# Reordering VectorE's sums at the seam between two MLP products, and the last rows' products and roots

## What is computed

```python
h = rmsnorm(x, g_pre_mlp[i]) * (1.0 + scale_f) + shift_f
y = jnp.square(jax.nn.relu(h @ w_mlp_in)) @ w_mlp_out      # 2048 -> 8192 -> 2048
x = x + gate_f * rmsnorm(y, g_post_mlp[i])
```

## Time and profile before

| | us |
|---|---|
| Median of 3 runs (lowest, highest) | 2253.55 (2251.96, 2254.7) |
| The profiled execution: device time | 2250.02 |
| Its span in the profile | 2248.2 |
| Mean granted TensorE clock | 0.986 |
| Busy: TensorE / VectorE / ScalarE / GpSimd | 2162.1 / 1511.6 / 862.5 / 391.1 |
| Second MLP product begins (first half of P1) | 1611.66 |
| Tail on VectorE: start of moving P5 out, end of the last row | 2225.19, 2243.72 |

### The profile page before, as it was taken

How to read it: one execution, slowest core, us unless ns; L and a number is a source line. 1 busy time by engine, 2 the same in 40 slices (tenths; PEclk the granted TensorE clock), 3 DMA queues, 4 the chain that set the end, 5 groups by cost and what they waited for, 6 DMA issues and landing times.

```text
span 2248.2 us, 26316 instructions
## 1 busy us (share of the span) xinstructions
PE 2162.1 (96%) x9751; PEld 1766.1 (79%) x9751; DVE 1511.6 (67%) x1459; ACT 862.5 (38%) x1076; POOL 391.1 (17%) x217
## 2 busy tenths in 40 slices
PE   4789999999999998999999999999999999999996
PEld 3568888887777887788888888888788888888875
DVE  6967666666767634665445444544688989898998
ACT  6333333331333224444344335334434444344443
POOL 1000000000000001000000000000054545463654
PEclk9899999999999999999999999999999999999998
DMA  9946654753454352566666646746455664567663
GB/s 366 354 163 217 200 185 133 235 162 115 153 168 136 119 182 74 192 220 225 201 202 220 224 171 206 250 159 202 131 187 180 239 236 166 190 233 243 236 237 138
DMA packets 262305, 441.16 MB, mean 196 GB/s; under 512 B 18156, under 2 KB 110512, under 8 KB 256184
## 3 DMA queue, kind: packets, MB, share of 16 engines
q1 hardware_dynamic: 261376, 435.45, 57.6%
q10 hardware_dynamic: 824, 4.27, 0.5%
HBM read 379.88 MB, written 59.79 MB: 196 GB/s over the span
## 4 chain that ended last, share of the span: by engine, by line
PE 80%; issue 8%; DVE 5%; DMA 3%; ACT 1%; POOL 1%; DVEq 1%; SPq 1%; POOLq 0%; ACTq 0%
PE pair L730 25%; PE pair L732 25%; PE pair L731 25%; DVE am_acc L1749 3%; DMA am_item<-in_w_ada 2%; DVE v_op L1976 1%; PE pair L827 1%; DMA w_raw<-in_w_in 1%; PE pair L801 1%; DVEq L1748 1%; POOL v_raw L2198 0%; PE pair L818 0%; PE pair L1014 0%; PE pair L867 0%; PE pair L876 0%
## 5 line engine op out<-in xcount | busy, mean ns | idle before, releaser
L730 PE MATMUL pair<-in_hi,w_hi 128*128 128x512 f32 x1792 | 723.6, 404 | 7.8 <-DVE in_lo L1766 6.2
L732 PE MATMUL pair<-in_hi,w_lo 128*128 128x512 f32 x1792 | 701.9, 392 | 0.0
L731 PE MATMUL pair<-in_lo,w_hi 128*128 128x512 f32 x1792 | 701.0, 391 | 0.0
L1509 DVE TENSOR_TENSOR w_lo<-w_raw,w_hi 128x2048 fp32r<-128x2048 f32 (+1 forms) x142 | 292.1, 2057 | 405.4 <-ACT w_hi L1107 405.0
L1107 ACT ACTIVATE w_hi<-w_raw 128x2048 fp32r<-128x2048 f32 (+1 forms) x142 | 244.8, 1724 | 461.6 <-PE pair L732 418.4
L730 PEld LDWEIGHTS pair<-in_hi,w_hi 128*128 128x128 f32 x1792 | 338.6, 189 | 87.2 <-issue 18.6
L732 PEld LDWEIGHTS pair<-in_hi,w_lo 128*128 128x128 f32 x1792 | 337.7, 188 | 72.9
L731 PEld LDWEIGHTS pair<-in_lo,w_hi 128*128 128x128 f32 x1792 | 338.7, 189 | 70.0 <-issue 2.6
L730 PE MATMUL pair<-v_op,hid_r 128*128 128x512 f32 x896 | 350.0, 391 | 5.8 <-DVE hid_r L1952 4.5
L732 PE MATMUL pair<-v_op,hid_r 128*128 128x512 f32 x896 | 349.5, 390 | 0.0
L731 PE MATMUL pair<-v_op,hid_r 128*128 128x512 f32 x896 | 349.5, 390 | 0.0
(11 more groups left out here) (202 smaller groups left out, 1882.8 us busy)
## 6 DMA issues: line engine op xcount, KB each, us to landing
w_raw<-in_w_mlp_in SPq DMA_DIRECT2D x64, 1024.0 KB, 5.3
v_raw<-in_w_mlp_out SPq DMA_DIRECT2D x128, 512.0 KB, 5.0
hid_r<-hid_scratch SPq DMA_DIRECT2D x112, 512.0 KB, 6.5
hid_scratch<-hid_r SPq DMA_DIRECT2D x28, 1792.0 KB, 6.5
am_item<-in_w_ada SPq DMA_DIRECT2D x64, 512.0 KB, 7.7
w_raw<-in_w_in SPq DMA_DIRECT2D x128, 256.0 KB, 3.6
af_item<-in_w_ada SPq DMA_DIRECT2D x64, 512.0 KB, 4.8
w_raw<-in_w_in SPq DMA_DIRECT2D x128, 128.0 KB, 3.5
```

Of the source, the lines that this page charges most:

```text
L730: pe.matmul(dst, a[0], b[0], start=start, stop=False, skip_group_check=onto)
L731: pe.matmul(dst, a[0], b[1], start=False, stop=False, skip_group_check=onto)
L732: return pe.matmul(dst, a[1], b[0], start=False, stop=stop, skip_group_check=onto)
L1509: dve.tensor_tensor(w_lo[n][:, view], w_raw[n][:, view], w_hi[n][:, view].bitcast(F32), ALU.subtract)\
```

## The change

At the seam, on VectorE: part 1 of the low parts of `hid_r` (of block 15) comes ahead of the sums; half 5's split comes next. B11 - B12 and B22 - B12 are made in halves of 128x1024 by a new `seam_b12`, and `seam_sum` orders itself by a drain in place of a wait on `t_dve`. GpSimd's products for `y_t2` (columns 2 and 0) move from unit 14 to behind unit 15's sums, and a third one (column 3), which VectorE made, goes to GpSimd between the two roots. The roots of row blocks 2 and 3, and of 0 and 1, are made in pairs. In the tail `out_row(0, 2)` comes ahead of adding the last product P4, and the last squares of C12 may start one `add` earlier.

```diff
--- before.py
+++ after.py
@@ -1464,7 +1464,8 @@
                     .then_inc(o_sq, 1)
 
             def finished(u):
-                return (ev_x, u + 1), (ev_y, 2 * u + 2), (ev_y, 2 * u + 2), (ev_q, 2 * u + 3)
+                c12 = (ev_w, UNITS + 1) if u == UNITS - 1 else (ev_y, 2 * u + 2)
+                return (ev_x, u + 1), c12, (ev_y, 2 * u + 2), (ev_q, 2 * u + 3)
 
             SQUARES = []
             for dc, u in ((0, U_DC0), (1, UNITS - 1)):
@@ -1954,9 +1955,10 @@
                     if b == LAST and part == 0:
                         split_operand(3)
                         split_operand(4)
-                        b12_sums(0, False)
-                        seam_sum(0)
-                        split_operand(5)
+                if b == LAST:
+                    split_operand(5)
+                    seam_b12(0)
+                    seam_sum(0)
 
             for b in range(FBS):
                 for mm in range(MM_O if b == 0 else 0, MM_O):
@@ -1991,11 +1993,22 @@
                     dve.tensor_tensor(v_raw[q[B11]][:, :, :], v_raw[q[B11]][:, :, :], v_raw[q[B12]][:, :, :],
                                       ALU.subtract).then_inc(t_dve, 1)
 
+            def seam_b12(h, third=False):
+                q = raw_at[0]
+                b11, b12, b22 = [v_raw[q[role]][:, h, :] for role in (B11, B12, B22)]
+                if third:
+                    return dve.tensor_tensor(b12, b22, b12, ALU.subtract)
+                if h == 0:
+                    done, count = raw_arrived(0, B12)
+                    dve.wait_ge(done, count)
+                    dve.wait_ge(v_lo, product_end(P1))
+                return dve.tensor_tensor(b11, b11, b12, ALU.subtract)
+
             def seam_sum(h):
                 q = raw_at[0]
                 done, count = raw_arrived(0, B22)
                 dve.wait_ge(done, count)
-                dve.wait_ge(t_dve, 1)
+                dve.drain()
                 dve.tensor_tensor(v_sum[:, h, :], v_raw[q[B22]][:, h, :], v_raw[q[B11]][:, h, :], ALU.add)\
                     .then_inc(t_seam, 1)
 
@@ -2032,7 +2045,10 @@
                 elif p == P5:
                     dve.wait_ge(ev_w, u + 1)
                     dve.wait_ge(ev_q, 2 * u + 2)
-                    add(c12, False)
+                    if u == UNITS - 1:
+                        add(c12, False).then_inc(ev_w, 1)
+                    else:
+                        add(c12, False)
                     add(c22, False).then_inc(ev_y, 1)
                 elif u < UNITS - 1:
                     add(c21, False).then_inc(ev_q, 1)
@@ -2046,10 +2062,14 @@
                     gate_row(Q_GF + FBS // 2 - 1, FBS // 2 - 1, bank[3])
                     hidden(LAST)
                 elif i not in (4, 5):
+                    if i == 6:
+                        seam_b12(1).then_inc(t_dve, 1)
                     split_operand(i)
                 if i == 6:
                     seam_sum(1)
-                    b12_sums(0, True)
+                    seam_b12(0, True)
+                if i == 7:
+                    seam_b12(1, True).then_inc(t_dve, 1)
                 while i - 4 >= product_end(evicted) - 1:
                     add_product(evicted)
                     evicted += 1
@@ -2070,7 +2090,8 @@
                 evicted += 1
 
             def total(t):
-                dve.tensor_reduce(ss4[:, t:t + 1], ss[:, t * CG:(t + 1) * CG], AX_X, ALU.add).then_inc(o_ss, 1)
+                rows = ss[:, t * CG:(t + 2) * CG].rearrange("p (t c) -> p t c", t=2)
+                dve.tensor_reduce(ss4[:, t:t + 2], rows, AX_X, ALU.add).then_inc(o_ss, 1)
 
             def out_row(n, t):
                 x1 = v_raw[raw_at[UNITS][ROLE_OF_T[t]]]
@@ -2084,25 +2105,21 @@
 
             dve.wait_ge(o_sq, 12)
             total(2)
-            total(3)
             gain(y_t1[:, :, 3, :], 3)
-            dve.wait_ge(o_sq, 14)
-            gain(y_t2[:, :, 3, :], 3)
+            dve.wait_ge(o_mul, 2)
+            dve.drain()
+            dve.wait_ge(o_rstd, 1)
+            out_row(0, 2)
             add_product(7 * UNITS - 1)
-            dve.wait_ge(o_mul, 4)
+            out_row(1, 3)
+            dve.wait_ge(o_sq, 16)
+            total(0)
+            gain(y_t2[:, :, 1, :], 1)
+            dve.wait_ge(o_mul, 5)
             dve.drain()
             dve.wait_ge(o_rstd, 2)
-            out_row(0, 2)
-            for t in range(2):
-                dve.wait_ge(o_sq, 15 + t)
-                total(t)
-                part = y_t2[:, t, 1, :]
-                dve.tensor_tensor(part, part, gg[:, 512:1024], ALU.mult)
-            out_row(1, 3)
-            dve.drain()
-            for t in range(2):
-                dve.wait_ge(o_rstd, 3 + t)
-                out_row(2 + t, t)
+            out_row(2, 0)
+            out_row(3, 1)
 
 
         @block.gpsimd
@@ -2208,11 +2225,13 @@
                 if u == U_DC0 + 1:
                     times_gain(y_t1, 0, 4)
                     times_gain(y_t1, 2, 4)
-                    times_gain(y_t2, 2, 8)
-                    times_gain(y_t2, 0, 8)
-            for n, t in enumerate((2, 3, 0, 1)):
-                pool.wait_ge(o_ss, n + 1)
-                inverse_root(rstd[:, t:t + 1], ms[:, t:t + 1], ss4[:, t:t + 1], D).then_inc(o_rstd, 1)
+            times_gain(y_t2, 2, 8)
+            times_gain(y_t2, 0, 8)
+            pool.wait_ge(o_ss, 1)
+            inverse_root(rstd[:, 2:4], ms[:, 2:4], ss4[:, 2:4], D).then_inc(o_rstd, 1)
+            times_gain(y_t2, 3, 14)
+            pool.wait_ge(o_ss, 2)
+            inverse_root(rstd[:, 0:2], ms[:, 0:2], ss4[:, 0:2], D).then_inc(o_rstd, 1)
 
 
 # ---- launch: one core; inputs and outputs as the reference has them ----
```

## The result

| | before | after |
|---|---|---|
| Median of 20 runs each, side by side (lowest, highest) | 2252.26 (2250.53, 2255.11) | 2257.26 (2254.61, 2261.16) |
| Ratio, 95% interval | | 1.0021 [1.0015, 1.0027] |
| The profiled execution: device time, span | 2250.02, 2248.2 | 2258.51, 2256.7 |
| First half of P1 begins | 1611.66 | 1615.93 |

The ratio is +4.7 us (+3.4 to +6.1). The two profiled executions differ by 8.5, but 4.27 of it lie ahead of the first half of P1, where no instruction was changed; over this case's profiled executions that point lies anywhere from 1611.5 to 1618.7.

The account below looks back on a forecast made before the run. TensorE, busy for 96% of the span, was taken as the bound, so time can only be won in its waits or behind its last matmul. Seam +3.7, units -1.0, tail +0.4 make +3.1 us: 2253.55 to 2256.7, range 2251.5 to 2259.5.

Parts of the forecast that it names:

- half 4's stall: Seam: TensorE's 4.5 us wait on hid_r goes; half 8 then waits for VectorE to empty bank Q.
- (A): Seam, half 8's split: VectorE goes before GpSimd's fourth instruction, half 8 at 1641.2, seam +3.2 us.
- (B): Seam, half 8's split: GpSimd's fourth instruction goes first, half 8 at 1642.35, seam +4.3 us.
- the middle: Seam taken as +3.7 us, between (A) and (B); part of the main forecast, given 62%.
- The clock: Behind half 8's stall: TensorE at 1.2 GHz again costs 2.7 us, ends 1.5 and 3.4.
- Units 14 and 15: Moved GpSimd pair: 1.5 us of waits go, a new unit 15 wait costs 0.4 to 0.55; net -1.0 us.
- The tail: From P5's move out: +0.4 us taken, +0.9 if GpSimd precedes the first row, -0.2 if VectorE does.
- GpSimd has the turn: Tail: GpSimd's third product goes before the first row, rows end at 2244.6, +0.9 us.
- rival 3: GpSimd goes first at half 8's split and the tail's first row, 1.2 GHz costs 3.4: +4.9 us, 2258.5; 18%.
- within: Whole kernel: time within 0.2%, 4.5 us, of before; chance 0.70.
- slower: Whole kernel: time slower than before by over 0.2%, 4.5 us; chance 0.22.
- Rivals 1 and 2: Seam: half 8 not held by VectorE's chain, -7.9 us (7%); stall moves without clock fall or ties go well, -0.7 (13%).

Follow-up runs that it names:

- P2 first: Changed kernel, with P2 moved out right behind P1, ahead of the split of half 8, and P3 behind that split; 0.9999 of before.
- GpSimd held: Changed kernel, with GpSimd's four instructions of unit 0 only after P2 is out; 1.0003 of before.
- seam only: Kernel before, with the change's VectorE edits at the seam and nothing else; 1.0017 of before, median 2256.26 us against 2252.00.
- pair moved: Kernel before, with GpSimd's two products of y_t2 moved behind unit 15's sums and nothing else; 0.9999 of before.
- P4 by halves: P6 early, but ScalarE's split of half 12 waits for the first two of GpSimd's four instructions, not all; 0.9975 of before.
- rest only: Changed kernel with the seam as before, all other parts of the change kept; 1.0003 of before.
- seam new: seam only, plus ScalarE moving P1 and P3 out, P2 out before half 8's split, last half-sum behind it, P7's first half waiting for its half-sum, GpSimd later; 0.9999.
- all new: Changed kernel with seam new's seam, gate-row products as two 128x512 instructions each, third product on VectorE again; 0.9988 of before.
- P6 early: all new, with P6 moved out by VectorE in the idle time ahead of the split of half 9; 0.9984 of before.
- P6 early, GpSimd held: P6 early, with GpSimd's four instructions of unit 0 starting only after the split of half 9; 0.9993 of before.

## Why the prediction was right, point by point

- **Why half 4's stall goes, and where it turns up.** Right. `hid_r`'s low part began at 1624.33 less 4.27, which is 1620.06, the start used for the working. Halves 6 and 7 were to start at 1628.4 and 1633.1; they did at 1628.37 and 1633.04. Bank Q held half 8: "P2 first" changes only the order in which VectorE moves P2 and P3 out, and half 8 came 3.33 earlier.
- **The turns and the tie.** The working gave half 8 two times, (A) 1641.2 and (B) 1642.35, and it came at 1642.41, which is (B). The forecast took the middle, since the nearest tie of before had gone to VectorE. That tie was misread: VectorE's split had begun there at 1637.02 and GpSimd's fourth at 1637.08, so the one that began first had the turn. In the changed kernel it was GpSimd, by 0.01 at half 8 (1640.55 against 1640.56) and by 0.06 at the first row (2237.37 against 2237.43); in "GpSimd held", at the split of half 10, again GpSimd, by 0.06 (1644.66 against 1644.72, the split 2.28 long). By the Trainium skill, "SBUF — State Buffer", section "Who interferes with whom", issue order decides, and these four ties agree. The working did have GpSimd ahead at half 8, by 0.02 (1636.29 against 1636.31). Read so, it gives (B), though with a margin of hundredths, less than such a working can be trusted with. "GpSimd held" prices what GpSimd's turns cost half 8: 3.2 us.
- **The clock.** 2.7 was carried over from before. Half 8 to half 10 took 7.91 where two halves take 5.44: 2.5 (7.85 in "seam only": 2.4). Slightly over-priced, and the range of 1.5 to 3.4 was not too wide: see the last section.
- **Units 14 and 15.** -1.0 forecast, -1.03 after (573.14 to 572.11 from unit 1 to the last matmul), -0.99 in "pair moved" (572.15). The new wait in unit 15 costs 0.46 (0.69 between two starts where 0.23 is usual) and, with its slower first matmul, 0.54, inside the 0.4 to 0.55.
- **The tail.** This is the term that was mis-sized: +0.4 as a middle of +0.9 and -0.2. It measured +1.11 from the last matmul to the end. The chain that the text worked out for the case "GpSimd has the turn" was right step by step: last row done 19.4 after P5's move began (2244.6 less 2225.19), measured 19.65 (2252.21 less 2232.56).
- **The sum.** +3.1 forecast; +4.14 (unit 1) - 1.03 + 1.11 = +4.2 in the trace, +4.7 (3.4 to 6.1) in the ratio, +5.0 in the medians. Both ties went to GpSimd, so both signs by which rival 3 was to be known came (half 8 after 1642.3, the first row over 4 us), without that rival's longer clock: its +1.6, +0.9 and -1.0 with 2.5 for the clock give +4.0. So the runs bear out rival 3's ties (18%) rather than the middle (62%), and the forecast's clock rather than rival 3's. The forecast's mechanism and sign were right, inside its range; the middle of two ties that hang on the same thing, who is a few hundredths of a microsecond ahead, was the wrong value to take. That the time came within 0.6 (2256.7 forecast, 2257.26 measured) is in part luck: the forecast's base of 2253.55 lay 1.3 above the median of before beside it, and the change was 1.6 to 1.9 short. The ratio lies at the bound of 0.2%, where "within" (0.70) and "slower" (0.22) can't be told apart.
- **Rivals 1 and 2** are out: half 8 came 1.67 later, not 4.6 earlier, and the clock fell.

## What to carry to other kernels

When a stall is taken away, list what each of the next steps waits for, buffers and banks as well as operands, and when each was ready before: here the slack behind the stall was 1.0 us, three more waits (P2 out of Q, P6 out of Y, P7 out of Q) lay in a row behind it. The version that moved all three out in time got 8 us; "P4 by halves", in which P7's move still stood behind two splits but no longer waited for all of GpSimd's work, got 5.6. Moving a result out of a bank belongs into the idle time of its engine ahead of the next wait for an operand, not behind work that itself waits. And where two engines take turns on SBUF, look which one starts first, price a tie that hangs on hundredths at its dearer end, or make it impossible by a semaphore.

## What the runs showed that was not expected

- **The same stall costs different amounts of clock.** A wait of 4.84 between two starts at half 4 was followed by 12 matmuls at 0.50 in before (2.7 us lost) and by half as many in "rest only" (half 4 to half 6 in 6.92 against 8.15 in before). One of 4.58 at half 8 in "GpSimd held" cost 2.4. Behind waits of 2.2 to 3.6 at halves 8, 10 and 12 the clock fell too, for a loss of 1.6 to 1.7 each (7.04 in "seam new", 7.16 in "all new", 7.14 in "P2 first", 7.14 in "P6 early" and 7.17 in "P6 early, GpSimd held" for two halves of 5.44 in all). Behind one of 1.10 at half 12, in "P4 by halves", and behind one of 2.09 at half 7, after, it did not. Where the clock fell, a wait of 2.2 to 3.6 us was thus half again or nearly twice as dear as it looks, and each version with such a wall left paid that once more.
- **In before and after 1.2 GHz began while TensorE still stood idle** (the row of 1645.00 above; in before 1625.85 to 1627.10 was at 0.50), so the loss was on its way before the next operand came. Behind shorter waits it could come later: in "P6 early" half 12 began at 1648.30, at 2.4 GHz for the first five matmuls, and then ran at 1.2 GHz.

```profile
1648.30:1649.40 1.10, 1.10 (x5) 1.00 0.79 229
1649.50:1652.80 3.30, 3.30 (x9) 0.50 0.63 233
```

- **A COPY from PSUM beside GpSimd costs neither anything**: GpSimd's first instruction took 1.30 beside P6's COPY of 1.22 in "P6 early"; its fourth, with VectorE idle, took 1.29 in "P6 early, GpSimd held", and P6's COPY there, with GpSimd at rest, 1.22. So in this kernel GpSimd's work is best laid beside VectorE's rows that read PSUM.
